# Expert down weights loaded by pairs of experts instead of by halves of rows

## Chip, cores and metric

The kernel runs on one core of a Trainium2 chip. The metric is the device time of one execution in microseconds (us); lower is better. All data are float32.

## What is computed

A decoder trunk of two layers on 256 tokens of width 1024. Each layer adds a mixer (state-space branch and sparse attention), a cross-attention and a hierarchical mixture of experts, and only the last is touched here:

```
for g in range(MOE_GROUPS):                      # 4 groups of 8 experts
    hid = (jax.nn.silu(jnp.einsum('nd,edf->nef', t, w_gate_e[g]))
           * jnp.einsum('nd,edf->nef', t, w_up_e[g]))          # f = 256
    hid = hid * combine[:, g, :, None].astype(hid.dtype)
    out = out + jnp.einsum('nef,efd->nd', hid, w_down_e[g]).astype(F32)
```

A token is routed to one group and there to two of its eight experts. Each expert has gate and up weights of 1024 x 256 and down weights of 256 x 1024, so 1 MB for each of the three.

## The kernel before

The expert part runs in passes. A pass takes one group, with 32 token slots for each of its 8 experts (`S`), in two blocks `b` of four experts (`BE`). Each layer of this run has four passes: the first (`opened`), the second (`early_rows`), the third, and one in a loop over passes (`Fori`) whose count comes from the routing.

What a block does, in TensorE's order (`expert_pass`):

- Gate product (i = 0) and up product (i = 1), line 1263: for each of 8 row chunks k, the four experts j one after the other. The stationary operand has 32 columns, and expert j writes partitions 32j to 32j+31 of a bank, so the four sit side by side on four column groups of the array.
- VectorE and ScalarE make `hid` (128 slots x 256). Two transposes (line 1288) turn its column halves into `hidT`, and ScalarE copies them (line 1559).
- Down product, line 1306: for k = 0, 1 (the half of the 256 rows f), for n = 0, 1 (the half of the 1024 outputs), for the four experts j. Step k reads the buffer `drows[2 * b + k]`: `xs`, `scr` for block 0 and `qq`, `ga` for block 1. (In the second pass `mix_rows` stands for `xs`.) Semaphore `dn_s` rises when k = 0 is over, `ds_s` when each n of k = 1 is over.
- ScalarE copies the sums (line 1565, `yg`), TensorE scatters them back to tokens (line 1323), and VectorE adds them to `h` (line 2220). Before a new pass, VectorE makes the selection (lines 2127, 2196) and TensorE gathers tokens (line 1203). In the first pass the gather for the second is done inside block 1.

All weights are loaded by SP, in one queue, in the order of its program: for each block gate (G), up (U), and the two down buffers (D0, D1). G and U are 4 MB each and go to the two halves of `wring`; a new G may be issued only when the gate product of the block before has read its half (`gu_s`, line 680), likewise U. D0 waits for `dn_s` and D1 for `ds_s` of the pass before (line 671). Since SP waits in order, what is late in front holds everything behind it. Each down buffer is 2 MB: of all four experts of a block, the rows k * 128 to k * 128 + 127, one row of 4 KB for each partition and expert. Gate and up are laid out so that a partition reads 8 KB in one piece.

Of the kernel before, what the change touches and what calls it, by code (L numbers as in the profile page):

```python
# [23 lines left out]
P = 128  # L24
# [251 lines left out]
def trunk(nc, x, mem, w_in, w_ssd_o, w_attn_o, w_out, w_cq, w_ckv, w_co, w_group, w_router,  # L276
          w_gate, w_up, w_down, params, consts, gain_final, out):
    with ExitStack() as ctx:
# [142 lines left out]
        def spare_sums(st):  # L421
# [7 lines left out]
            if st[0] == "atto":  # L429
# [6 lines left out]
        drows = [xs[:, :, :].rearrange("p t (a n) -> p (t a) n", a=2), scr[:, :].rearrange("p (j n) -> p j n", j=BE),  # L436
                 qq[:, :, :].rearrange("p t (a n) -> p (t a) n", a=2), ga[:, :].rearrange("p (j n) -> p j n", j=BE)]
        fgain = cols(mix, 0, D)
        xg_ahead = cols(hT[:, :, :].rearrange("p c t -> p (c t)"), 0, KC, E * S)
        up_ahead = cols(big, 4096, KC * F)  # L440
        gate_ahead = cols(hT[:, :, :].rearrange("p c t -> p (c t)"), 0, KC * F)
# [99 lines left out]
        def drained(eng, l, job):  # L541

            eng.wait_ge(drained_s[OWNER[job]], l * DRAINS[OWNER[job]] + RANK[job])
# [32 lines left out]
        def group_of(engine, i):  # L576

            return number(engine, bass.ds(i, 1), 0, G - 1)
# [15 lines left out]
        def _(sp):  # L594
# [65 lines left out]
                row = acum_rows[l, t, g * HG:(g + 1) * HG, :].rearrange("h s -> (h s)")  # L660
                sp.dma_start(mm_[:, (n + 1) % 2, :], bc(row, 0, P)).then_inc(dec_in[n % 2], 16)

            def down(l, u, g, b, i):

                if i == 0:
                    sp.wait_ge(dn_s, u * NB + (b + 1))
                else:
                    sp.wait_ge(ds_s, u * (2 * NB) + (2 * b + 2))
                settle(sp)
                src = w_down[l, g, b * BE:(b + 1) * BE].rearrange("j (k p) n -> p k j n", p=P)  # L670
                sp.dma_start(drows[2 * b + i][:, :, :], src[:, i]).then_inc(d_in_sem[2 * b + i], 16)

            def up(l, u, g, b, i, first=0):

# [4 lines left out]
                src = (w_gate, w_up)[i][l, g, b * BE:(b + 1) * BE].rearrange("j (p k) n -> p j (k n)", p=P)  # L679
                sp.dma_start(up_part[i][:, first:BE, :], src[:, first:BE, :]).then_inc(up_part_in[i], 16)  # L680

            def experts(l, u, g, down_ahead=(), opening=False):

                for b in range(NB):
                    for i in range(PARTS):
                        if opening and b == 0 and i == 1:

                            sp.wait_ge(gu_s, u * (PARTS * NB) + (i + 1))
                            settle(sp)
                            src = w_up[l, g, 0:BE].rearrange("j (p k) n -> p j (k n)", p=P)  # L690
                            for half, got in enumerate((up_half_in, up_part_in[i])):
                                filled(sp, l, last_job(NCH - PARTS + half))
                                settle(sp)
                                js = slice(half * (BE // 2) + 1 - half, (half + 1) * (BE // 2))
                                if half:
                                    sp.dma_start(up_part[i][:, js, :], src[:, js, :]).then_inc(got, 16)
                                    continue
                                after = w_up[l, g, BE].rearrange("(p k) n -> p (k n)", p=P)
                                sp.dma_start(up_part[i][:, 0, :], after).then_inc(up_next_in, 16)
                                sp.dma_start(up_part[i][:, js, :], src[:, js, :]).then_inc(got, 16)  # L700
                            down(l, u, g, 1, 0)
                            filled(sp, l, JOB[(("router", 1), 0)])
                            settle(sp)
                            after = w_gate[l, g, BE].rearrange("(p k) n -> p (k n)", p=P)
                            sp.dma_start(gate_ahead, after).then_inc(gate_ahead_in, 16)
                            continue
                        if opening and b == 1 and i == 0:

                            src = w_gate[l, g, BE:2 * BE].rearrange("j (p k) n -> p j (k n)", p=P)
                            for half, got in enumerate((gate_half_in, up_part_in[i])):  # L710
                                if half == 0:
                                    sp.wait_ge(gate_half_used, l + 1)
                                else:
                                    sp.wait_ge(gu_s, u * (PARTS * NB) + (PARTS * b + i + 1))
                                settle(sp)
                                ks = slice(half * (KC // 2) * F, (half + 1) * (KC // 2) * F)
                                sp.dma_start(up_part[i][:, 1:BE, ks], src[:, 1:BE, ks]).then_inc(got, 16)
                            continue

                        if not (opening and b == 0):  # L720
                            up(l, u, g, b, i, first=int(opening))
                    for i in range(2):
                        if (b, i) not in down_ahead:
                            down(l, u, g, b, i)

            before = 0
            for l in range(DEPTH):
                sp.wait_ge(prm_used, l + 1)
                settle(sp)
                sp.dma_start(prm[:, :], params[l]).then_inc(prm_in, 16)  # L730
                z0 = CHUNK[(("z", 0), 0)]
                ahead_of = {z0 + 2: (0,), z0 + 4: (1, 2), z0 + 5: (3, 4), z0 + 6: (5, 6), z0 + 7: (7,)}
                for c in range(NCH):
                    if c == CHUNK[(("xbc", 4), 0)]:
                        save_acum(l)
                    for n in ahead_of.get(c, ()):
                        acum_to_all(l, n)
                    chunk(l, c, before)
                    if c == CHUNK[(("cq", 0), 0)]:

                        filled(sp, l, JOB[(("memT", 3), 0)])
                        settle(sp)
                        src = w_down[l, 1, 0:BE].rearrange("j (k p) n -> p k j n", p=P)
                        sp.dma_start(mix_rows, src[:, 0]).then_inc(mix_in, 16)

                        drained(sp, l, JOB[(GATES[3], 4)])
                        settle(sp)
                        sp.dma_start(rw[:, :, 0:G], rows(w_group[l], 0, G)).then_inc(router_in, 16)
                        sp.dma_start(rw[:, :, G:G + G * E], rows(w_router[l], 0, G * E)).then_inc(router_in, 16)

                filled(sp, l, last_job(CHUNK[(("cv", 1), 0)]))
                settle(sp)
                sp.dma_start(up_ahead, w_up[l, 0, 0].rearrange("(p k) n -> p (k n)", p=P)).then_inc(up_ahead_in, 16)
                filled(sp, l, last_job(CHUNK[(("cq", 1), 0)]))
                settle(sp)
                down(l, before, 0, 0, 0)
                up(l, before, 0, 0, 0)
                filled(sp, l, JOB[(("xpv", 3), 0)])
                settle(sp)
                drained(sp, l, JOB[(("cq", 1), 4)])  # L760
                settle(sp)
                down(l, before, 0, 0, 1)
                down(l, before, 0, 1, 1)
                experts(l, before, 0, down_ahead=[(0, 0), (0, 1), (1, 0), (1, 1)], opening=True)
                down(l, before + 1, 1, 0, 1)
                for i in range(1, PLAIN):
                    experts(l, before + i, i, down_ahead=[(0, 0), (0, 1)] if i == 1 else [])
                if l == DEPTH - 1:

                    sp.wait_ge(dn_s, (before + 2) * NB + 1)  # L770
                    settle(sp)
                    sp.dma_start(fgain, gain_final).then_inc(fin_in, 16)
                total, after = passes(sp, SP, l)
                with sp.Fori(PLAIN, total) as i:
                    experts(l, before + i, group_of(SP, i))
                before = after
            for t in range(TT):
                sp.wait_ge((fin_act, fin_s)[t], 1)
# [59 lines left out]
        def _(pe):  # L838
# [379 lines left out]
                    if c % 2:  # L1218
                        ins.then_inc(gat_s, 1)

            def expert_pass(u, spared, opened=False, early_rows=False):

                x = xg_ahead if early_rows else xg
                if opened:
# [8 lines left out]
                for b in range(NB):  # L1233
# [50 lines left out]
                    pe.wait_ge(hid_s, u * NB + (b + 1))  # L1284
                    if opened and b == 0:
                        drained(pe, l, JOB[(("count",), 0)])
                    for k in range(2):
                        ins = nc.tensor.transpose(bank[3][:, k * P:(k + 1) * P], hid[:, b, k * P:(k + 1) * P], ident)
                    ins.then_inc(hT_s, 1)
                    pe.wait_ge(hTc_s, u * NB + (b + 1))  # L1290
                    if opened and b == 1:
# [3 lines left out]
                    for k in range(2):  # L1295
# [6 lines left out]
                        else:  # L1302
                            pe.wait_ge(d_in_sem[0], (u + 1 - spared) * 16)
                        for n in range(2):
                            for j in range(BE):
                                ins = nc.tensor.matmul(bank[4 + n][j * S:(j + 1) * S, :],  # L1306
                                                       hidT[:, b, k * P + j * S:k * P + (j + 1) * S],
                                                       rows[:, j, n * NCOL:(n + 1) * NCOL], start=k == 0, stop=k == 1)
                            if k:
                                ins.then_inc(ds_s, 1)  # L1310
                        if k == 0:
# [16 lines left out]
            for l in range(DEPTH):  # L1328
# [6 lines left out]
                expert_pass(before + 2, l + 1)  # L1335
                total, after = passes(pe, PE, l)
                with pe.Fori(PLAIN, total) as i:
                    expert_pass(before + i, l + 1)
                before = after


# [974 lines left out]
```

## Time and profile before

| | us |
|---|---|
| median of 3 runs | 1497.06 (1496.94 to 1497.62) |
| profiled execution | 1496.66 |
| its span in the trace | 1494.9 |
| TensorE busy | 1376.9 (92%) |
| granted clock, mean | 0.976 of full |
| weights and other HBM reads | 355.89 MB, 239 GB/s over the span |

The span is 1.8 us shorter than the execution's own time. Busy shares are means over stages that differ: in the slices 14 to 19 and 34 to 39 (of 40, counted from 0) the expert passes run, at about 415 GB/s, and in the others products of TensorE bound the kernel. The order of a layer is mixer, cross-attention, experts, so the expert parts lie at about 536 to 743 us and 1275 to 1484 us of the span.

### The profile page before, as it was taken

What the parts mean: (1) busy time and instruction counts of PE and PEld (TensorE: products, weight loads), DVE (VectorE), ACT (ScalarE), POOL (GpSimd) and SP (SyncE); (2) the same over time, 40 slices, a digit from 0 to 9 for tenths busy, and PEclk for the clock granted to TensorE, in tenths of its full rate; (3) what the DMA queues carried; (4) which work ended last, traced back from release to release, by engine and by line L of the source; (5) the groups of instructions that cost most, each with busy time, mean ns of one, the idle gap of its engine ahead of it and who ended that gap; (6) DMA issues with size and microseconds to landing.
All of it is one profiled execution on the core that took longest, in us unless ns stands there. A gap on an engine that the chain in (4) does not pass through costs nothing.

```text
span 1494.9 us, 23994 instructions
## 1 busy us (share of the span) xinstructions
PE 1376.9 (92%) x9670; PEld 1095.7 (73%) x9670; DVE 842.3 (56%) x1605; ACT 383.5 (26%) x867; POOL 70.1 (5%) x65
## 2 busy tenths in 40 slices
PE   8999999999999999767699999999999999978674
PEld 7888888899999654424288888889999996534241
DVE  5477878796875342112265878787958653322022
ACT  2222567421111111001122235576111021111001
POOL 0000420000000000000000014100000000000000
PEclk9999999999999999989999999999999999998998
DMA  9434443353663789999963455433346646999996
GB/s 318 164 119 178 169 156 113 114 197 114 226 229 111 312 352 390 417 415 417 389 223 124 159 183 173 152 114 127 128 149 214 217 187 266 395 389 415 418 417 245
DMA packets 119102, 358.56 MB, mean 240 GB/s; under 512 B 12112, under 2 KB 14544, under 8 KB 103376
## 3 DMA queue, kind: packets, MB, share of 16 engines
q1 hardware_dynamic: 118448, 354.93, 62.6%
q8 instruction: 78, 1.28, 0.4%
q0 software_dynamic: 544, 2.10, 0.4%
q14 instruction: 32, 0.26, 0.1%
HBM read 355.89 MB, written 1.11 MB: 239 GB/s over the span
## 4 chain that ended last, share of the span: by engine, by line
PE 79%; DMA 16%; DVE 2%; issue 1%; SPq 0%; ACT 0%; DVEq 0%; POOL 0%; POOLq 0%; ACTq 0%
PE bank L920 21%; PE bank L923 18%; PE bank L889 13%; DMA ga<-in_w_down_e 11%; DMA wring<-in_w_up_e 5%; PE bank L870 5%; PE bank L1263 5%; PE bank L1203 4%; PE bank L844 3%; PE bank L1040 2%; PE bank L1323 2%; PE bank L1306 1%; PE bank L1129 1%; PE bank L1116 1%; PE bank L1065 1%
## 5 line engine op out<-in xcount | busy, mean ns | idle before, releaser
L889 PE MATMUL bank<-hT,wring 128*128 128x256 f32 x896 | 196.2, 380 | 0.0
L889 PEld LDWEIGHTS bank<-hT,wring 128*128 128x128 f32 x896 | 169.3, 190 | 23.9 <-issue 0.7
L1263 PE MATMUL bank<-wring,big 128*32 128x256 f32 x1472 | 100.7, 421 | 34.7 <-DMA wring<-in_w_up_e 19.9
L2220 DVE TENSOR_TENSOR h<-bank,h 128x512 f32<-128x512 f32 x64 | 44.3, 692 | 116.7 <-PE bank L1323 116.7
L1263 PEld LDWEIGHTS bank<-wring,big 128*32 128x32 f32 x1472 | 50.2, 121 | 76.0 <-DMA wring<-in_w_up_e 22.1
L1816 DVE SCALAR_TENSOR_TENSOR scr<-bank,prm,scr 128x255 f32<-128x255 f32 (+1 forms) x144 | 62.7, 477 | 46.8 <-ACT scr L1389 44.0
L2211 DVE TENSOR_TENSOR big<-bank,big 128x256 f32<-128x256 f32 x16 | 6.8, 425 | 143.9 <-ACT big L1555 143.9
L920 PE MATMUL bank<-hT,wring 128*128 128x128 f32 x736 | 86.9, 276 | 0.8 <-DVE btok L1673 0.8
L920 PEld LDWEIGHTS bank<-hT,wring 128*128 128x128 f32 x736 | 84.2, 192 | 3.4 <-issue 2.1
L1203 PE MATMUL bank<-big,xn 128*128 128x256 f32 x256 | 72.5, 439 | 12.5 <-DVE big L2127 12.3
L1354 ACT ACTIVATE ga<-bank 128x256 f32<-128x256 f32 x48 | 18.4, 384 | 247.6 <-PE bank L920 173.0
L1203 PEld LDWEIGHTS bank<-big,xn 128*128 128x128 f32 x256 | 65.5, 335 | 22.0 <-DVE big L2127 16.0
L920 PE MATMUL bank<-big,wring 128*128 128x128 f32 x704 | 80.9, 275 | 0.0
L920 PEld LDWEIGHTS bank<-big,wring 128*128 128x128 f32 x704 | 79.9, 192 | 0.1
L923 PE MATMUL bank<-wring,hT 128*128 128x256 f32 x336 | 77.1, 379 | 0.0
L923 PE MATMUL bank<-wring,xn 128*128 128x256 f32 x320 | 72.3, 379 | 0.0
L923 PEld LDWEIGHTS bank<-wring,hT 128*128 128x128 f32 x336 | 63.5, 190 | 11.0 <-issue 2.9
L923 PEld LDWEIGHTS bank<-wring,xn 128*128 128x128 f32 x320 | 60.6, 190 | 11.6 <-issue 3.8
L1323 PE MATMUL bank<-big 128*128 128x512 f32 x128 | 62.2, 618 | 0.1
L1643 DVE TENSOR_TENSOR wring<-wring 128x1024 f32<-128x1024 f32 (+1 forms) x44 | 59.6, 1354 | 1.2
L870 PE MATMUL bank<-wring,qq 128*128 128x512 f32 x128 | 56.9, 595 | 0.0
L1555 ACT ACTIVATE big<-bank 128x256 f32<-128x256 f32 x16 | 6.2, 385 | 192.4 <-PE bank L1263 192.4
(370 smaller groups left out, 2333.6 us busy)
## 6 DMA issues: line engine op xcount, KB each, us to landing
wring<-in_w_in SPq DMA_DIRECT2D x68, 1024.0 KB, 7.2
wring<-in_w_gate_e SPq DMA_DIRECT2D x14, 4096.0 KB, 18.1
wring<-in_w_up_e SPq DMA_DIRECT2D x12, 4096.0 KB, 23.6
wring<-in_w_ssd_o SPq DMA_DIRECT2D x16, 1024.0 KB, 6.2
wring<-in_w_ckv SPq DMA_DIRECT2D x16, 1024.0 KB, 7.3
scr<-in_w_down_e SPq DMA_DIRECT2D x8, 2048.0 KB, 22.6
ga<-in_w_down_e SPq DMA_DIRECT2D x8, 2048.0 KB, 29.2
qq<-in_w_down_e SPq DMA_DIRECT2D x8, 2048.0 KB, 24.7
```

The source lines that it names most:

```text
L844: ins = nc.tensor.transpose(b[:, i * P:(i + 1) * P], src, ident)
L870: ins = nc.tensor.matmul(bank[bank_of(job)][:, 0:width], src[:, k, t * P:(t + 1) * P], wring[:, SLOT[c], k, 0:width], start=i == 0, stop=i ...
L889: ins = nc.tensor.matmul(bank[bank_of(job)][:, i * SEQ:(i + 1) * SEQ], wring[:, SLOT[c], k, m:m + P], src[:, k, :], start=n == 0, stop=n = ...
L920: ins = nc.tensor.matmul(b[:, i * P:(i + 1) * P], w[:, j, i * P:(i + 1) * P], x[:, j, :], start=j == 0, stop=j == k - 1)
L923: ins = nc.tensor.matmul(b[:, 0:HALF_W], x[:, j, :], w[:, j, :], start=j == 0, stop=j == k - 1)
L1040: ins = nc.tensor.matmul(bank[bank_of(job)][:, i * SP_:(i + 1) * SP_], mm_[:, (n + 1) % 2, i * P:(i + 1) * P], xdt[:, n % 2, i * SP_:(i + ...
L1203: return nc.tensor.matmul(bank[banks[c // 2]][:, (c % 2) * E * S:(c % 2 + 1) * E * S], xn_eighth[:, k, c, :], sel[:, k, :], start=start, s ...
L1263: ins = nc.tensor.matmul(bank[b][j * S:(j + 1) * S, i * F:(i + 1) * F], x[:, k, e:e + S], w[:, k * F:(k + 1) * F], start=k == 0, stop=k == ...
L1323: nc.tensor.matmul(bank[6 + n][:, :], selT[:, b, k * P:(k + 1) * P], yg[:, n * NCOL:(n + 1) * NCOL], start=True, stop=True).then_inc(sct_s, 1)
L1643: V.tensor_tensor(out, a, b, ALU.subtract).then_inc(wsum_rdy, 1)
L1816: ins = V.scalar_tensor_tensor(conv[:, m % 2, i, k:SEQ], b[:, i * SEQ:(i + 1) * SEQ - k], prm[:, w:w + 1], conv[:, m % 2, i, k:SEQ], ALU.m ...
L2220: V.tensor_tensor(hh, bank[6 + n][:, :], hh, ALU.add).then_inc(add_s, 1)
```

## The change

Down weights now come by pairs of experts. Buffer `drows[2 * b + i]` holds the whole down weights of the experts 2i and 2i+1 of its block, and partition p holds rows 2p and 2p+1 of each, which lie one behind the other in memory: 8 KB in one piece. The same 2 MB go to the same buffer at the same place of SP's order. Only block 1 of the looped pass keeps the old form.

On TensorE the transposes take every second column of `hid` instead of the first and second 128. Step k of the down product now does the whole of two experts: for each n, row half 0 for both, then row half 1 for both. Block 1 of the looped pass keeps the old order.

```diff
+        def pair_rows(rows):
+            return rows.rearrange("p (j k) n -> p j (k n)", k=2)
...
+            def down_pair(l, g, b, i):
+                e = b * BE + 2 * i
+                return w_down[l, g, e:e + 2].rearrange("j (p k) n -> p j (k n)", p=P)
...
-            def down(l, u, g, b, i):
+            def down(l, u, g, b, i, pairs=True):
...
-                src = w_down[l, g, b * BE:(b + 1) * BE].rearrange("j (k p) n -> p k j n", p=P)
-                sp.dma_start(drows[2 * b + i][:, :, :], src[:, i]).then_inc(d_in_sem[2 * b + i], 16)
+                if pairs:
+                    dst, src = pair_rows(drows[2 * b + i]), down_pair(l, g, b, i)
+                else:
+                    dst = drows[2 * b + i][:, :, :]
+                    src = w_down[l, g, b * BE:(b + 1) * BE].rearrange("j (k p) n -> p k j n", p=P)[:, i]
+                sp.dma_start(dst, src).then_inc(d_in_sem[2 * b + i], 16)
...
-                            down(l, u, g, b, i)
+                            down(l, u, g, b, i, pairs=not (looped and b))
...
-                        src = w_down[l, 1, 0:BE].rearrange("j (k p) n -> p k j n", p=P)
-                        sp.dma_start(mix_rows, src[:, 0]).then_inc(mix_in, 16)
+                        sp.dma_start(pair_rows(mix_rows), down_pair(l, 1, 0, 0)).then_inc(mix_in, 16)
...
+                    pairs_in = not (looped and b)
                     for k in range(2):
-                        ins = nc.tensor.transpose(bank[3][:, k * P:(k + 1) * P], hid[:, b, k * P:(k + 1) * P], ident)
+                        part = hid[:, b, :].rearrange("p (q k) -> p k q", k=2)[:, k] if pairs_in else hid[:, b, k * P:(k + 1) * P]
+                        ins = nc.tensor.transpose(bank[3][:, k * P:(k + 1) * P], part, ident)
...
-                            for j in range(BE):
+                            steps = ([(2 * k + a, j, 2 * a + j) for j in range(2) for a in range(2)] if pairs_in
+                                     else [(j, k, j) for j in range(BE)])
+                            for j, half, row in steps:
                                 ins = nc.tensor.matmul(bank[4 + n][j * S:(j + 1) * S, :],
-                                                       hidT[:, b, k * P + j * S:k * P + (j + 1) * S],
-                                                       rows[:, j, n * NCOL:(n + 1) * NCOL], start=k == 0, stop=k == 1)
+                                                       hidT[:, b, half * P + j * S:half * P + (j + 1) * S],
+                                                       rows[:, row, n * NCOL:(n + 1) * NCOL], start=half == 0, stop=half == 1)
```

On SP, from the down load that the first pass triggers to the two of the second pass, before (4 experts x 1024 elements for each partition in a down load):

```order
L671 DMA scr<-in_w_down_e 128x4x1024
L680 DMA wring<-in_w_gate_e 128x4x2048
L680 DMA wring<-in_w_up_e 128x4x2048
L680 DMA wring<-in_w_gate_e 128x4x2048
L680 DMA wring<-in_w_up_e 128x4x2048
L671 DMA qq<-in_w_down_e 128x4x1024
L671 DMA ga<-in_w_down_e 128x4x1024
```

and now:

```order
L685 DMA scr<-in_w_down_e 128x2x2048
L694 DMA wring<-in_w_gate_e 128x4x2048
L694 DMA wring<-in_w_up_e 128x4x2048
L694 DMA wring<-in_w_gate_e 128x4x2048
L694 DMA wring<-in_w_up_e 128x4x2048
L685 DMA qq<-in_w_down_e 128x2x2048
L685 DMA ga<-in_w_down_e 128x2x2048
```

No load has moved; each down load has half as many pieces, twice as long.

On TensorE, the down product and the scatter of the first pass's block 0, before:

```order
L1288 MATMUL bank3<-cst,big 128x128 x2
L1306 MATMUL bank4<-xs,big 32x512 x4
L1306 MATMUL bank5<-xs,big 32x512 x4
L1306 MATMUL bank4<-scr,big 32x512 x4
L1306 MATMUL bank5<-scr,big 32x512 x4
```

and now:

```order
L1303 MATMUL bank3<-cst,big 128x128 x2
L1323 MATMUL bank4<-xs,big 32x512 x4
L1323 MATMUL bank5<-xs,big 32x512 x4
L1323 MATMUL bank4<-scr,big 32x512 x4
L1323 MATMUL bank5<-scr,big 32x512 x4
```

The count of products and their banks are the same. What the rows don't show is that each group of four went to the column groups 0, 1, 2, 3 before and goes to 0, 1, 0, 1 (`xs`) and 2, 3, 2, 3 (`scr`) now.

## Rows read from the trace of the kernel before

**Rows 1.** The page's 40 slices of the span, in tenths; last row the moved GB/s.

```profile
PE   8999999999999999767699999999999999978674
...
GB/s 318 164 119 178 169 156 113 114 197 114 226 229 111 312 352 390 417 415 417 389 223 124 159 183 173 152 114 127 128 149 214 217 187 266 395 389 415 418 417 245
```

**Rows 2.** Chain that ended last, layer 0: start us, us, engine, line; matmuls and weight loads counted.

```profile
547.84 3.64 PE bank L1306 x32
...
566.71 17.52 DMA wring<-in_w_up_e
...
644.02 33.38 DMA ga<-in_w_down_e
```

**Rows 3.** PE, first pass: start us, us, line, out<-in, form, count [idle before <-releaser].

```profile
547.84 1.92 PE L1306 MATMUL bank<-xs,big 128*32 128x512 f32 x16 [0.47 <-ACT big L1559]
549.58 1.90 PE L1306 MATMUL bank<-scr,big 128*32 128x512 f32 x16
551.43 3.87 PE L1323 MATMUL bank<-big 128*128 128x512 f32 x8
...
571.93 1.92 PE L1306 MATMUL bank<-qq,big 128*32 128x512 f32 x16 [0.98 <-ACT big L1559]
573.68 1.90 PE L1306 MATMUL bank<-ga,big 128*32 128x512 f32 x16
...
579.33 3.66 PE L1263 MATMUL bank<-wring,hT 128*32 128x256 f32 x64
```

**Rows 4.** PE in order of time: a product on two column groups.

```profile
253.09 1.08 PE L1085 MATMUL bank<-qq,mix 128*64 128x512 f32 x4
```

**Rows 5.** Windows of 2 us: us, busy of PE, PEld, DVE, ACT, POOL; clock, DMA share, GB/s.

```profile
580.00:582.00 2.00, 2.00 (x44) 1.23 (x40) 0.89 (x3) 0.00 (x0) 0.00 (x0) 1.00 0.87 365
582.00:584.00 2.00, 1.58 (x24) 0.75 (x16) 0.39 (x1) 0.00 (x0) 0.00 (x0) 1.00 0.23 90
584.00:586.00 2.00, 1.73 (x32) 1.07 (x36) 0.31 (x1) 0.00 (x0) 0.00 (x0) 1.00 0.92 254
```

**Rows 6.** The queue of SP, issues of weight loads: start us, us, line.

```profile
559.01 0.37 SPq L680 DMA_DIRECT2D wring<-in_w_gate_e  x1
...
583.11 0.37 SPq L680 DMA_DIRECT2D wring<-in_w_gate_e  x1
...
701.97 0.37 SPq L680 DMA_DIRECT2D wring<-in_w_gate_e  x1
...
1322.82 0.37 SPq L680 DMA_DIRECT2D wring<-in_w_gate_e  x1
...
1440.22 0.37 SPq L680 DMA_DIRECT2D wring<-in_w_gate_e  x1
```

**Rows 7.** Windows as in rows 5, in streams of gate/up (1, 3) and down (2, 4).

```profile
708.00:724.00 16.00, 10.98 (x104) 4.07 (x99) 2.76 (x4) 1.20 (x2) 0.00 (x0) 1.00 1.01 421
726.00:734.00 8.00, 5.67 (x66) 2.58 (x66) 0.42 (x1) 0.39 (x1) 0.00 (x0) 0.70 1.02 409
1448.00:1464.00 16.00, 10.76 (x92) 4.02 (x88) 2.77 (x4) 1.20 (x2) 0.00 (x0) 0.89 1.01 419
1468.00:1476.00 8.00, 6.16 (x74) 2.86 (x78) 0.42 (x1) 0.77 (x2) 0.00 (x0) 0.79 1.03 410
```

**Rows 8.** Weight loads by line and form: busy us, mean ns, idle before.

```profile
L1203 PEld LDWEIGHTS bank<-big,xn 128*128 128x128 f32 x256 | 65.5, 335 | 22.0 <-DVE big L2127 16.0 <-issue 3.3
L1288 PEld LDWEIGHTS bank<-cst,big 128*128 128x128 f32 x32 | 3.4, 142 | 20.4 <-DVE big L2211 20.3
```

**Rows 9.** PE in order of time: down product of the third pass, block 1, both layers.

```profile
675.45 1.92 PE L1306 MATMUL bank<-qq,big 128*32 128x512 f32 x16 [0.47 <-ACT big L1559]
677.44 1.92 PE L1306 MATMUL bank<-ga,big 128*32 128x512 f32 x16
...
1413.98 1.92 PE L1306 MATMUL bank<-qq,big 128*32 128x512 f32 x16 [0.47 <-ACT big L1559]
1417.22 1.92 PE L1306 MATMUL bank<-ga,big 128*32 128x512 f32 x16 [1.32 <-DMA ga<-in_w_down_e]
```

More of the change, by code:

```diff
@@ L680, in up, with experts @@
                 sp.dma_start(up_part[i][:, first:BE, :], src[:, first:BE, :]).then_inc(up_part_in[i], 16)
-            def experts(l, u, g, down_ahead=(), opening=False):
+            def experts(l, u, g, down_ahead=(), opening=False, looped=False):
                 for b in range(NB):
@@ L774, in _ @@
                 with sp.Fori(PLAIN, total) as i:
-                    experts(l, before + i, group_of(SP, i))
+                    experts(l, before + i, group_of(SP, i), looped=True)
                 before = after
@@ L1219, in gather_both, with expert_pass @@
                         ins.then_inc(gat_s, 1)
-            def expert_pass(u, spared, opened=False, early_rows=False):
+            def expert_pass(u, spared, opened=False, early_rows=False, looped=False):
                 x = xg_ahead if early_rows else xg
@@ L1337, in _ @@
                 with pe.Fori(PLAIN, total) as i:
-                    expert_pass(before + i, l + 1)
+                    expert_pass(before + i, l + 1, looped=True)
                 before = after
```

## Prediction

> **What bounds the kernel now.** I read the page's slices first. The expert parts (slices 14 to 19 and 34 to 39) move about 415 GB/s and every other part moves far less [rows 1]. There the DMA engines look like the bound, and the change shortens pieces of just these loads. But the change also rearranges the down product on TensorE, so the second question is where in the expert part TensorE is the bound. The chain that ended last answers it: from 547.84 to 566.7 us it is TensorE's alone, then it goes over to landings of gate, up and down weights, with waits of 17 to 33 us [rows 2]. So a layer's expert part has two regimes. In the first pass, whose weights were mostly loaded ahead, TensorE runs from product to product. From the second pass on the stream of 24 MB a pass decides.
>
> The seam between the two is where the price of this change is set. SP may issue the gate load of the second pass's block 1 only after the gate product of that pass's block 0, which runs from 579.33 to 583.0 [rows 3], and the issue stands at 583.11 [rows 6]. By then the queue has run dry: the DMA share is 0.87, 0.23 and 0.92 in the three windows of 2 us from 580 on [rows 5]. Taking the missing shares, that is 2.0 us of nothing. So here the stream waits for TensorE: whatever makes TensorE later in the first pass makes this issue later, and all that comes behind, up to the last down load of the layer, is one stream that then has no more gap to take it up. This is the point at which a microsecond of TensorE is a microsecond of the kernel.
>
> **Pieces of 8 KB.** The last two down loads of a layer run alone, in pieces of 4 KB: 409 and 410 GB/s. Streams of gate and up alone, in pieces of 8 KB: 421 and 419 GB/s [rows 7]. 2 MiB are 2.097 MB: 5.12 us at 409.5, 4.99 us at 420, so a down load saves 0.13 us (from 421 against 409, 0.15; from 419 against 410, 0.11). Behind the seam, eight changed down loads per layer follow: qq and ga of the second pass, four of the third, xs and scr of the looped one. 8 x 0.13 = 1.05 us per layer. The loads before the seam (four for the first pass, two for the second's first block) are hidden: TensorE decides there. Two layers: **-2.1 us**, bounds -1.8 and -2.4.
>
> A rule speaks against even this. The Trainium skill, "DMA: Bandwidth & Descriptors", Specifications, puts the least size for line rate at 512 B, so that 4 KB and 8 KB would do the same. Rows 7 disagree by 2.5%; going by the rule the saving would be nothing.
>
> **The down product on half the array.** Before, the four experts of a block stand on four column groups and run side by side. The trace shows it: 16 instructions of 512 columns take 1.92 us, and step k = 1 starts 1.74 us after k = 0 (547.84 to 549.58, [rows 3]), so four rounds of 4 instructions, 0.43 us a round. Now step k holds two experts, in the order a, b, a, b. Equal groups must follow each other, so a round is 2 instructions and there are 8 rounds a step. The trace has such a product: on two column groups, 4 instructions of 512 columns take 1.08 us [rows 4], which is two rounds of 0.43 and a tail. So 8 rounds are 3.47 us instead of 1.74, and a block with both steps costs 16 rounds, +3.47 us. At the seam of the two steps the groups differ (0, 1, then 2, 3), so the second step may start beside the last round of the first: up to 0.3 us back. I take **+3.3 us per block**; bounds: 1.7 (if half of it overlaps, for which no row speaks) and 3.5.
>
> Where does it count? In the first pass both blocks' down products lie in the unbroken run of TensorE: 547.84 and 571.93 [rows 3]; behind each, scatter, products and gather follow with no idle time over 1 us, and none of them for a load. 2 x 3.3 = 6.6 us later at the seam. One step earlier the same delay meets the gate load at 559.01 [rows 6]; it comes 3.3 us later and starves the stream some 2 us, but the loads behind it end at 584 or so, before the new issue at 583.1 + 6.6 = 589.7, so it isn't added. The gap at the seam grows from 2 us to about 8.6. **+6.6 us per layer, +13.2 in both** (the same issue stands at 1322.82 in layer 1 [rows 6]). In the later passes TensorE waits for loads soon after a down product, and behind block 0's product the next G is issued with both down loads of block 1 and most of U still ahead of it in the queue: over 10 us of stream at 420 GB/s, against 3.3 us. So nothing there.
>
> **The looped pass's seam.** The one later place that is tight is the same issue one pass on: the gate load of block 1 in the looped pass. Layer 0: the third pass's last down load lands at 644.02 + 33.38 = 677.4 [rows 2]. Landing is seen about 2 us after the queue ends with it. Behind it G, U, xs, scr are queued, 12.6 MB, 30.2 us at 416. A new load needs 1.7 us to flow (583.11 to about 584.8, [rows 5, 6]). So the new G must be issued by 677.4 - 2.0 + 30.2 - 1.7 = 703.9; it is at 701.97 [rows 6]: 1.9 us of slack. The third pass's block 1 starts its two steps at 675.45 and 677.44 [rows 9]; with 3.47 us each, they end 3.0 us later than now. 1.1 us are short, and the faster xs and scr take 0.3 more: the stream waits 1.2 us or so, bounds 0 and 1.6. Layer 1: steps at 1413.98 and 1417.22 [rows 9], so k = 0 is just over when the second load lands, and only +1.8 us remain, against a slack of 1417.2 - 2.0 + 30.2 - 1.7 - 1440.22 = 3.5. Nothing. **+1.2 us.** The last block of the layer keeps the old order, so the tail behind the last landing stays.
>
> **Transposes.** They now read every second column of `hid` as stationary operand, two per block, on TensorE's path in the first pass. The trace has no such load. The contiguous ones of now have a mean of 142 ns; the gather's loads, which take every eighth column, 335 ns [rows 8]. So between nothing and 4 x 0.19 = 0.8 us per layer (two blocks, two exposed each). I take 0, since a step of two columns is nearer to one than to eight; bound +1.5 in both layers.
>
> The Trainium skill, "SBUF — State Buffer", the note on cachelines under "Door 1: The DMA port swizzle", says lines of 16 bytes with two hits in each run at full rate. A stride of two floats has two hits, the gather's one; rows 8 agree for the latter, and no row here shows the former. By that rule the transposes cost 0, as in the sum.
>
> **Sum.** Against the profiled execution of 1496.66 (span 1494.9), 0.4 us below the median: -2.1 + 13.2 + 1.2 = +12.3 us. On the median of 1497.06: **1509.4 us**, own range 1506 to 1513 from the bounds without the overlap.
>
> **Rivals.**
> 1. TensorE overlaps the two row halves of an expert in part, so that a block costs 1.7 us. Then the seam moves 3.4 us a layer, the looped pass's seam nothing: 6.8 - 2.1 = +4.7, 1501.8 us. Against it: rows 4, where alternate groups take full rounds.
> 2. The down product costs nothing at the seam, since something else that I take for idle sets the gate issue. Then only the pieces count: -2.1, 1495.0 us, which is within 0.2%; to be faster by over 3 us a load would have to save 0.19 us, half as much again as rows 7 give. That decides if the issue at 583.11 doesn't move. Against it: it follows the product's end by 0.1 us in the trace.
> 3. Pieces of 8 KB bring nothing for these loads, as if they were moved as 4 KB: no -2.1, 1511.5 us. Against it: rows 7. It is what the rule above from the Trainium skill, "DMA: Bandwidth & Descriptors", would give.
> 4. The pass seams get worse than summed: strided transposes at the upper bound, the looped seam short in both layers and a lower clock after the longer waits: +3 to +5 more, 1513 to 1515 us.
>
> **Chances.** Forecast 0.67, rival 1 0.10, rival 2 0.09 (of it 0.03 faster), rival 3 0.08, rival 4 0.06. A measurement of this kernel tells about 0.2% (3 us) from no change. Slower 0.91, same 0.06, faster 0.03. The range leaves out rival 2 and the most of rival 4: 1501 to 1513.
>
> **What would show it.** In the changed profile: the 16 down instructions of `xs` take about 3.6 us instead of 1.92; block 0's scatter in the first pass starts near 554.8 and block 1's near 582; the second pass's second gate issue stands at about 589.7, with the DMA share near zero for 8 us ahead of it; behind it, streams of down loads at 420 GB/s; the chain holds TensorE up to 573 instead of 566.7. The forecast is wrong if the down product of 16 instructions stays under 2.5 us, or if that gate issue stays at 583.

## The result, and the profile after

| | us | lowest to highest; of the ratio, 95% interval |
|---|---|---|
| before, median of 7 | 1497.06 | 1495.98 to 1497.62 |
| after, median of 7 | 1501.74 | 1500.95 to 1503.28 |
| ratio after / before | 1.0033 | 1.0024 to 1.0042 |
| profiled execution, after | 1501.32 (span 1499.5) | |

The kernel became slower by 4.7 us, 0.33%. The direction was forecast, the size was not: 12.3 us were. The median lies below the own range of 1506 to 1513 us, and at the very foot of the wide one of 1501 to 1513, which only rival 1 reached.

TensorE in order of time around the down product of the first pass's block 0, after the change (start us, us, engine, line, form, count; line 1323 is the down product, 1340 the scatter):

```profile
549.05 2.34 PE L1323 MATMUL bank<-xs,big 128*32 128x512 f32 x10 [0.47 <-ACT big L1576]
550.80 0.62 PE L1323 MATMUL bank<-scr,big 128*32 128x512 f32 x2
551.22 0.60 PE L1323 MATMUL bank<-xs,big 128*32 128x512 f32 x2
551.26 0.60 PE L1323 MATMUL bank<-scr,big 128*32 128x512 f32 x2
552.08 0.60 PE L1323 MATMUL bank<-xs,big 128*32 128x512 f32 x2
552.12 2.31 PE L1323 MATMUL bank<-scr,big 128*32 128x512 f32 x10
554.36 1.98 PE L1340 MATMUL bank<-big 128*128 128x512 f32 x4
```

This answers to [rows 3]. The products of `xs` (experts 0 and 1) start at 549.05 and those of `scr` (experts 2 and 3) already at 550.80, 1.75 us later, while `xs` still goes on, two instructions a round, until 552.08 and a round more. From 550.80 on two on `xs` and two on `scr` run beside each other. The scatter starts 5.31 us after the first product, where it was 3.59 us before: a block costs +1.7 us, not +3.3.

The queue of SP, the gate loads that answer to [rows 6]:

```profile
561.96 0.37 SPq L694 DMA_DIRECT2D wring<-in_w_gate_e  x1
587.82 0.37 SPq L694 DMA_DIRECT2D wring<-in_w_gate_e  x1
...
1328.96 0.37 SPq L694 DMA_DIRECT2D wring<-in_w_gate_e  x1
```

From the first down product (549.05) to the second gate issue of the second pass (587.82) are 38.77 us. Before, it was 583.11 - 547.84 = 35.27 [rows 3, 6]: +3.50 us, of which the two blocks' products make 1.72 and 1.73. The chain of waits gives the same stations (start us, us, engine, line), after:

```profile
549.05 5.38 PE bank L1323 x32
554.43 3.82 PE bank L1340 x8
...
588.30 3.63 PE bank L1276 x64
592.00 19.38 DMA wring<-in_w_up_e
...
741.61 1.92 PE bank L1323 x16
...
1289.94 5.38 PE bank L1323 x32
...
1483.33 1.92 PE bank L1323 x16
```

and before:

```profile
737.60 1.92 PE bank L1306 x16
...
751.55 10.78 PE bank L870 x64
...
1287.26 3.64 PE bank L1306 x32
...
1478.55 1.92 PE bank L1306 x16
```

In layer 1 the same stretch is 1328.96 - 1289.94 = 39.02 against 1322.82 - 1287.26 = 35.56 [rows 6]: +3.46 us. The chain stays with TensorE until 592.00, where it left it at 566.71 [rows 2] and 573 were forecast. Before, TensorE reached the up product of that block 0.70 us ahead of its load's landing (584.27), and so the chain went back along that load:

```profile
584.27 3.66 PE L1263 MATMUL bank<-wring,hT 128*32 128x256 f32 x64 [0.70 <-DMA wring<-in_w_up_e]
```

Now TensorE comes after the landing.

From the second gate issue to the product behind the last landing of the layer: 741.61 - 587.82 = 153.79 against 737.60 - 583.11 = 154.49, so -0.70 us; in layer 1 154.37 against 155.73, -1.36 us. There the saving of the longer pieces is seen.

Windows after the change (us, busy of PE, PEld, DVE, ACT, POOL, clock, DMA share, GB/s):

```profile
584.00:586.00 2.00, 2.00 (x37) 1.20 (x40) 1.45 (x3) 0.00 (x0) 0.00 (x0) 1.00 0.17 70
586.00:588.00 2.00, 2.00 (x35) 1.14 (x28) 0.00 (x0) 0.00 (x0) 0.00 (x0) 1.00 0.04 12
588.00:590.00 2.00, 2.00 (x39) 1.15 (x41) 0.69 (x1) 0.00 (x0) 0.00 (x0) 1.00 0.49 135
670.00:678.00 8.00, 5.85 (x66) 2.98 (x66) 0.42 (x1) 0.48 (x2) 0.00 (x0) 0.79 1.02 424
712.00:728.00 16.00, 13.30 (x106) 5.01 (x106) 3.11 (x5) 1.58 (x3) 0.00 (x0) 1.00 1.01 424
708.00:712.00 4.00, 3.44 (x64) 1.82 (x56) 0.66 (x2) 0.38 (x1) 0.00 (x0) 1.00 1.02 369
```

Three things answer to [rows 5] and [rows 7]. The queue is dry for longer at the first pass's seam: shares of 0.17, 0.04 and 0.49 in three windows of 2 us, 4.6 us without load in these alone. Down loads are no longer told from gate and up loads: 424 GB/s from 670 to 678, in front of the landing at 681.0 of the third pass's last down load, and 424 from 712 on, where gate and up load. And there is a short gap at the looped pass's seam in layer 0, 369 GB/s from 708 to 712.

**What of the profile is no part of the change.** The first product of the layer's experts stands 1.21 us later than before (549.05 against 547.84), though nothing before it was changed but how a few loads are cut. Of this, 0.07 us are the strided transposes (experiment 3). In the five experiments whose code is the same up to there (all but 2 and 3) the product stands between 547.94 and 548.94, so the most of it is a difference between executions. And the start of layer 1 came 1.3 us earlier, against the product behind the last landing: before, its first large product is at 751.55 (13.95 us behind 737.60), after, at

```profile
754.25 10.72 PE bank L883 x64
```

12.64 us behind 741.61. Here the granted clock tells why. Before:

```profile
748.00:752.00 4.00, 3.90 (x21) 3.88 (x22) 1.75 (x4) 1.25 (x4) 0.00 (x0) 0.60 1.05 387
```

and after, in the same stretch of the program:

```profile
752.00:756.00 4.00, 3.69 (x32) 3.51 (x32) 1.66 (x4) 2.72 (x5) 0.00 (x0) 1.00 1.05 387
```

0.60 is a mean over 4 us between the two levels, 1.2 and 2.4 GHz. Before the window TensorE had waited for VectorE and ScalarE (1.61 us busy out of 4 in the window before, after the change 1.62), and in one execution the clock fell there and in the other it did not; what decides it, these rows don't show. Of the seven experiments' profiled executions one has the short stretch too, that of experiment 6, with a granted clock of 1.00 there; the six others have the long one, with 0.57 to 0.66 over the 4 us in question. So +1.2 and -1.3 cancel to 0.1, and the difference of the profiled executions, 4.66 us, is made by 3.50 - 0.70 + 3.46 - 1.36 = 4.9 us, less 0.2 at the end.

### The profile page after: what moved, and what is told of

Its sections match the earlier page's. It is cut to its first block, busy times and chain, and to the rows that moved or that the text cites. A ratio compares the mean times of both kernels' runs of the same rounds, so it can differ in the third digit from the quotient of the medians.

```text
span 1499.5 us, 23994 instructions
## 1 busy us (share of the span) xinstructions
PE 1403.0 (94%) x9670; PEld 1106.2 (74%) x9670; DVE 842.5 (56%) x1605; ACT 383.0 (26%) x867; POOL 71.1 (5%) x65
## 4 chain that ended last, share of the span: by engine, by line
PE 85%; DMA 10%; DVE 3%; issue 1%; ACT 1%; DVEq 0%; SPq 0%; POOL 0%; ACTq 0%; POOLq 0%
PE bank L933 21%; PE bank L936 18%; PE bank L902 13%; PE bank L1276 6%; DMA wring<-in_w_up_e 6%; PE bank L883 5%; PE bank L1216 5%; DMA ga<-in_w_down_e 4%; PE bank L1323 3%; PE bank L857 3%; PE bank L1340 3%; PE bank L1053 2%; PE bank L1142 1%; PE bank L1129 1%; PE bank L1078 1%
## 5 line engine op out<-in xcount | busy, mean ns | idle before, releaser
L1216 PE MATMUL bank<-big,xn 128*128 128x256 f32 x256 | 72.4, 439 | 12.5 <-DVE big L2144 12.3
L801 POOL TENSOR_TENSOR sums<-sums,cst 128x2 f32<-128x2 f32 (+2 forms) x13 | 10.6, 818 | 937.9 <-DVE sums L1613 353.4
```

Of the source, the lines that this page charges most:

```text
L1216: return nc.tensor.matmul(bank[banks[c // 2]][:, (c % 2) * E * S:(c % 2 + 1) * E * S], xn_eighth[:, k, c, :], sel[:, k, :], start=start, s ...
```

## Experiments

All are edits of the changed kernel. Medians are compared with the 1501.74 of the changed kernel and the 1497.06 of the one before, whose medians beside the experiments were 1497.06 (1 to 4) and 1496.98 (5 to 7). The ratios are to these, with a 95% interval.

### 1. Four column groups in each round

```diff
+                    if pairs_in:
+                        ... # waits for both loads of the block
+                        for n in range(2):
+                            for half in range(2):
+                                for e in range(BE):
+                                    rows = mix_rows if early_rows and b == 0 and e < 2 else drows[2 * b + e // 2]
+                                    ins = nc.tensor.matmul(bank[4 + n][e * S:(e + 1) * S, :],
+                                                           hidT[:, b, half * P + e * S:half * P + (e + 1) * S],
+                                                           rows[:, 2 * (e % 2) + half, n * NCOL:(n + 1) * NCOL],
+                                                           start=half == 0, stop=half == 1)
```

> The changed kernel, but where down weights come by pairs the product waits for both loads of a block and then goes through all four experts for each row half, so that each round stands on four column groups again. Theory A (the loss comes from the down product of the first pass's two blocks on two groups at a time): a block's 32 instructions take 3.6 us as before the change instead of 5.4, the second pass's second gate issue comes back by 3.5 us relative to the start of the layer's expert part, and the pieces' saving of 2.1 us is left: 1495.0 us, 1493.5 to 1496.5. Theory B (the loss comes from the new layout itself, such as the loads' landing or the strided transposes): the time stays near 1501.5 us.

Measured: 1496.32 us (1495.37 to 1497.92, 11 runs), ratio to before 0.9994 (0.9985 to 1.0003). TensorE in the first pass, and the gate issue of the seam:

```profile
548.20 0.62 PE L1322 MATMUL bank<-xs,big 128*32 128x512 f32 x2 [0.47 <-ACT big L1595]
548.21 0.62 PE L1322 MATMUL bank<-scr,big 128*32 128x512 f32 x2
...
551.23 0.60 PE L1322 MATMUL bank<-xs,big 128*32 128x512 f32 x2
551.24 0.60 PE L1322 MATMUL bank<-scr,big 128*32 128x512 f32 x2
551.77 1.55 PE L1359 MATMUL bank<-big 128*128 128x512 f32 x3
...
583.47 0.37 SPq L694 DMA_DIRECT2D wring<-in_w_gate_e  x1
```

Two instructions on `xs` and two on `scr` start together from the first round on, the scatter follows after 3.57 us, and the gate issue is 583.47 - 548.20 = 35.27 us behind the first product, in layer 0 to the hundredth as before the change (in layer 1 35.68 against 35.56). So the seam's whole delay sits in these products. The time is 1.3 us above what I expected, inside the range, and the trace shows one reason: with both loads waited for, the looped pass's seam of layer 0 is dry for longer, a share of 0.93 and 338 GB/s in

```profile
704.00:708.00 4.00, 3.81 (x66) 1.98 (x64) 0.69 (x1) 0.13 (x1) 0.00 (x0) 1.00 0.93 338
```

so that from the second gate issue to the product behind the last landing it saves 0.0 us in layer 0 (737.94 - 583.47 = 154.47, against 154.49), but 1.4 us in layer 1 (154.37 against 155.73).

### 2. The first pass in the old form

```diff
-                down(l, before, 0, 0, 0)
+                down(l, before, 0, 0, 0, pairs=False)
...
-                    pairs_in = not (looped and b)
+                    pairs_in = not (looped and b or opened)
```

(and so for the first pass's three other down loads.)

> The changed kernel, with the four down loads and the two down products of the first pass in the old form (4 KB pieces, four groups). Theory A: only these two blocks cost time, the blocks of the later passes are hidden behind loads: 1495.0 us, 1494 to 1497, and the second pass's second gate issue stands where it did before the change. Theory B (the later passes lose as well, by products that end 1.8 us later behind the last landing and by a queue that runs dry in the looped pass): 1498 to 1500 us.

Measured: 1495.10 us (1493.23 to 1497.18, 11 runs), ratio 0.9987 (0.9978 to 0.9996). Theory A. The first pass's product and the gate issue of the seam:

```profile
548.36 1.92 PE L1323 MATMUL bank<-xs,big 128*32 128x512 f32 x16 [0.47 <-ACT big L1576]
...
583.63 0.37 SPq L694 DMA_DIRECT2D wring<-in_w_gate_e  x1
```

That is 35.27 us again, as before the change. With the first pass alone taken back, 6.6 us come back, and what is left of the change is a gain of 2.0 us: what pieces of 8 KB save where loads bound the kernel, less what the later passes' new order costs there.

### 3. Pairs in pieces of 4 KB

```diff
-                return w_down[l, g, e:e + 2].rearrange("j (p k) n -> p j (k n)", p=P)
+                return w_down[l, g, e:e + 2].rearrange("j (k p) n -> p (j k) n", p=P)
...
-            return rows.rearrange("p (j k) n -> p j (k n)", k=2)
+            return rows
...
-                        part = hid[:, b, :].rearrange("p (q k) -> p k q", k=2)[:, k] if pairs_in else hid[:, b, k * P:(k + 1) * P]
+                        part = hid[:, b, k * P:(k + 1) * P]
```

> The changed kernel with its pairs of experts and its order of products, but each buffer takes the rows k * 128 + p, in pieces of 4 KB, and the transposes are contiguous again. Theory A (pieces of 8 KB save 0.13 us a load behind the seam, transposes cost nothing): 1501.7 + 2.1 = 1503.8 us, 1503 to 1505. Theory B (pieces make no difference): 1501.7. Theory C (strided transposes cost more than the pieces save): under 1501 us.

Measured: 1504.33 us (1503.62 to 1504.67, 5 runs), ratio 1.0046 (1.0032 to 1.0060). Theory A: the order of products alone costs 7.3 us, and pieces of 8 KB, with the strided transposes that come with them, give 2.6 us of it back (2.1 expected). Behind the seam this kernel takes what the one before took, 154.49 us in layer 0 and 155.67 in layer 1 (154.49 and 155.73), so there the order of products alone costs nothing that the trace shows, and what the changed kernel saves there is by its pieces. The same run prices the strided transposes. Contiguous, here (line 1303 is the transposes):

```profile
548.10 0.44 PE L1303 MATMUL bank<-cst,big 128*128 128x128 f32 x2 [0.96 <-DVE big L2228]
549.01 2.34 PE L1323 MATMUL bank<-xs,big 128*32 128x512 f32 x10 [0.47 <-ACT big L1576]
550.76 0.62 PE L1323 MATMUL bank<-scr,big 128*32 128x512 f32 x2
```

0.91 us from the transposes to the first product; strided, in the changed kernel, weight loads of this line have a mean of 197 ns instead of 142 [rows 8], 28 of the 32 being strided (so about 205 ns for a strided one; in experiment 7, where all 32 are, the mean is 206):

```profile
L1303 PEld LDWEIGHTS bank<-cst,big 128*128 128x128 f32 x32 | 5.0, 197 | 20.3 <-DVE big L2228 20.3
```

and the way takes 0.98 us (548.07 to 549.05). So 0.07 us for block 0 of a first pass. Block 1's transposes lie beside a wait for ScalarE's copies and cost nothing: from the first down product to the seam's gate issue are 38.78 us with contiguous ones and 38.77 with strided ones. That makes 0.14 us in both layers. The Trainium skill, "SBUF — State Buffer", the note on cachelines under "Door 1: The DMA port swizzle", would have had a stride of two floats cost nothing; the measurement says some 60 ns a load, small, but not nothing.

### 4. Step 1 only after step 0

```diff
+                        if opened and k:
+                            pe.wait_ge(dn_s, u * NB + (b + 1) + NB)
```

> The changed kernel, and in the first pass step 1 of a block's down product waits until step 0 is over. Theory A (in the changed kernel step 1 starts on its own two groups 1.75 us after step 0, while half of step 0 still waits for its groups, and so a block costs 1.75 us instead of 3.4): a block now takes 7.1 us instead of 5.4, each layer's seam moves by another 3.4 us: 1501.7 + 6.9 = 1508.6 us, 1507 to 1510. Theory B (a block's time is set otherwise, and the steps' overlap is only how the trace models ends): 1501.7 us.

Measured: 1510.49 us (1509.60 to 1511.42, 4 runs), ratio 1.0091 (1.0075 to 1.0106).

```profile
548.05 3.63 PE L1325 MATMUL bank<-xs,big 128*32 128x512 f32 x16 [0.47 <-ACT big L1578]
551.84 3.63 PE L1325 MATMUL bank<-scr,big 128*32 128x512 f32 x16 [0.16 <-PE bank L1325]
555.40 3.89 PE L1342 MATMUL bank<-big 128*128 128x512 f32 x8
...
590.87 0.37 SPq L694 DMA_DIRECT2D wring<-in_w_gate_e  x1
```

This is the kernel that the prediction had priced: steps one after the other, each of 8 rounds, 3.63 us. A block takes 7.35 us to the scatter instead of 5.31, so 2.04 us more, of which 1.7 are the overlap and 0.3 the wait itself. Four blocks make 8.2 us; by medians 8.75 were measured, 0.5 us above the range, and between the profiled executions (1509.60 and 1501.32) 8.3. With the overlap forbidden the loss against before is 13.4 us, near the 13.2 + 1.2 - 2.1 = 12.3 of the prediction. So theory A's cause holds, though its range was missed by the wait's own price: what the sum lacked is that step 1 starts on its own two groups while step 0 still waits for its groups.

### 5. One expert after the other

```diff
+                        if opened:
+                            for a in range(2):
+                                for n in range(2):
+                                    for half in range(2):
+                                        e = 2 * k + a
+                                        ins = nc.tensor.matmul(...)   # as before, on group e
```

> The changed kernel, and in the first pass a step goes through one expert after the other: 8 instructions on one column group, then 8 on the next. Theory A1 (each column group holds three instructions that wait for it, and TensorE goes past them to other groups): an expert's products start four rounds of 0.43 us after those of the one before, at 0, 1.74, 3.47 and 5.2 us, and a block takes 8.9 us instead of 5.4; two blocks in two layers: +13.9 us, 1515.6 us, 1513 to 1518. Theory A2 (six may wait in all, whatever their group): starts at 0, 0.4, 2.2 and 3.9 us or so, a block takes about 7.4 us, 1509.7 us. Theory A3 (TensorE goes past nothing that waits): a block takes 13.9 us, 1535 us.

Measured: 1515.46 us (1515.26 to 1515.89, 4 runs), ratio 1.0123 (1.0108 to 1.0139).

```profile
547.94 4.08 PE L1324 MATMUL bank<-xs,big 128*32 128x512 f32 x13 [0.47 <-ACT big L1587]
551.43 0.62 PE L1324 MATMUL bank<-scr,big 128*32 128x512 f32 x1
551.85 0.59 PE L1324 MATMUL bank<-xs,big 128*32 128x512 f32 x1
...
552.71 0.59 PE L1324 MATMUL bank<-xs,big 128*32 128x512 f32 x1
552.74 4.05 PE L1324 MATMUL bank<-scr,big 128*32 128x512 f32 x13
556.73 3.46 PE L1351 MATMUL bank<-big 128*128 128x512 f32 x7
```

Expert 2 (the first on `scr`) starts at 551.43, 3.49 us behind expert 0 (3.47 by theory A1, 2.2 by A2), and the products end 8.85 us after the first starts (8.9 by A1). The rows from 551.43 to 552.71 also show expert 1's and expert 2's products side by side, one and one. Expert 1 is merged with expert 0 in the first row; narrower views have one instruction on `xs` at 549.25 and two from 549.68 on, 1.74 us behind the first, again as in A1 (0.4 by A2). So in these runs TensorE goes past an instruction that waits for a busy column group, and each group holds three that wait; the fourth stops everything behind it. One limit for all groups together doesn't fit both kernels: here three wait when the next group's first gets by, in the changed kernel six. The three is worked out from these starts; what in TensorE holds them, the runs don't show. In the changed kernel that is just what sets 1.75 us: a step has 8 instructions for each of its groups, and the ninth, the other step's first, gets by when the eighth is among the three that wait, which is when the fifth starts, four rounds in.

### 6. Four groups in the first pass only

Experiment 1 with `if opened:` in place of `if pairs_in:`, so that the later passes are those of the changed kernel.

> The changed kernel, pairs and 8 KB everywhere as there, but in the first pass alone the product goes through four experts for each row half. Theory A: the seam of the first pass is that of the kernel before, and behind it all is as in the changed kernel: 3.5 us less per layer, 1501.7 - 7.0 = 1494.7 us, 1493.5 to 1496, so the same as with the first pass in halves (1495.1). Theory B (the later passes with steps on two groups cost more than with four groups, or the other way): away from 1494.7 by over 1 us, towards 1496.3, which four groups everywhere gave.

Measured: 1494.75 us (1493.92 to 1496.92, 11 runs), ratio 0.9988 (0.9979 to 0.9997). The lowest median here; it and experiment 2 (1495.10) are the only ones faster than before beyond the interval, by 2.2 and 2.0 us. It is also 1.6 us under experiment 1, whose later passes wait for both loads of a block before the first product; the samples of the two overlap, so how much of the 1.6 us that waiting costs is not settled. In the profiled executions layer 0 behind the seam takes 153.26 us here and 154.47 there, and experiment 1's window shows the place.

### 7. Pairs in the looped pass's block 1 too

```diff
-                            down(l, u, g, b, i, pairs=not (looped and b))
+                            down(l, u, g, b, i, pairs=True)
...
-                    pairs_in = not (looped and b)
+                    pairs_in = True
```

> The changed kernel, with the looped pass's block 1 in pairs too. Theory A: behind the last landing of a layer stand 8 rounds on two groups instead of 4 on four, +1.73 us, and two more loads save 0.13 us each, so +1.5 us per layer and 1501.7 + 3.0 = 1504.7 us, 1503.5 to 1506. Theory B (the tail is hidden behind the scatter and the next layer's first work): 1501.7 or 0.5 us less.

Measured: 1504.43 us (1504.24 to 1505.96, 5 runs), ratio 1.0051 (1.0038 to 1.0065). The end of layer 0:

```profile
738.19 2.34 PE L1323 MATMUL bank<-qq,big 128*32 128x512 f32 x10 [0.47 <-ACT big L1576]
740.22 0.62 PE L1323 MATMUL bank<-ga,big 128*32 128x512 f32 x2
...
741.54 2.31 PE L1323 MATMUL bank<-ga,big 128*32 128x512 f32 x10
743.78 3.95 PE L1340 MATMUL bank<-big 128*128 128x512 f32 x8
```

Behind the last landing (740.22) the scatter starts after 3.56 us, where the old form has 1.93 (741.61 to 743.54 in the changed kernel). These products lie on the chain that ended last, so all of it counts: 2.7 us in both layers, with the saving of four more loads taken off. This is what the exception for that block avoids.

## Why the prediction was right in direction and wrong in size

- **Where the price is set: right.** The second gate issue of the second pass moved by 3.50 and 3.46 us, of which the two blocks' products of the first pass make 3.45 and 3.40, and it went through to the end of each layer. Experiments 2 and 6, which touch the first pass alone, bring it back to 35.27 and 35.26 us in layer 0 (35.27 before).
- **The down product on half the array: the term that was mis-sized.** The step "at the seam of the two steps the groups differ, so the second step may start beside the last round of the first: up to 0.3 us back" took the overlap for one round. It is four rounds: a block costs 1.7 us, not 3.3, so 7.0 us in all instead of 13.2. [rows 4] showed rightly that two groups take full rounds, but its four instructions could not show what stands in the queue behind them. The bound of 1.7 was in the text, tied to an overlap of row halves; experiment 4 shows that it is the overlap of the steps. Rival 1 had the time (1501.8) for the wrong cause, and a chance of 0.10. The prediction's signs did not test the overlap: 16 instructions on `xs` do take 3.6 us, as it said, and neither sign of being wrong came, yet the seam's gate issue stood 38.77 us behind the first product where about 41.9 were forecast, and its queue was dry for some 4.6 us, not 8.6.
- **Pieces of 8 KB: right, somewhat more than summed.** -1.36 us in layer 1 against -1.05, or 0.17 us a load instead of 0.13 (0.15 to 0.17 in experiments 1, 2, 4, 5 and 6); by medians 2.6 us between experiment 3 and the changed kernel. The Trainium skill, "DMA: Bandwidth & Descriptors", Specifications, asks only for 512 B, and by that 4 KB and 8 KB would run alike; these runs don't bear that out, nor rival 3.
- **The looped pass's seam: right in place, its size not settled.** In the changed kernel's trace layer 0 saves 0.66 us less than layer 1, and a window of it shows 369 GB/s; 1.2 us were forecast, within bounds of 0 to 1.6 (its two parts, 1.1 and 0.3, make 1.4). Layer 1 shows no such loss, as forecast. But experiments 2, 4, 5 and 6, whose later passes are the same, save 0.58, 1.03, 0.98 and 1.23 us in layer 0 in one execution each, so the loss lies between nothing and 0.8 us and differs by execution. With pieces of 4 KB (experiment 3) there is none.
- **Transposes:** 0.14 us, between the bounds of 0 and 1.5.
- **Rival 4** adds up to 1512.4 to 1514.4 us, not 1513 to 1515; nothing hangs on it.
- With the sizes of the profiled executions the sum is 7.0 - 2.7 + 0.7 + 0.1 = 5.1 us, against 4.7 measured.

## What to carry to other kernels

A change that makes transfers cheaper and products dearer is to be judged stage by stage: here it gained 2 us where loads bound the kernel and lost 7 us in the one pass where TensorE bound it, and either form of the repair (the old layout there, or four column groups there) left the gain alone. When products stand on separate column groups of the array, price them by the longest run of instructions on one group and by what may pass them, not by rounds put end to end; and keep neighbouring instructions on different groups. In front of a last landing keep the form whose products behind it are shortest.

## What the runs showed of the hardware that was not expected

- TensorE's instructions for a free column group pass those that wait for a busy one, until three wait for a group. The second step started 1.75 us after the first (four rounds of 0.43 us) with six instructions of the first still to run; with one group at a time, the second expert started 1.74 us and the third 3.49 us after the first. So products do not start in the order of the program.
- A semaphore wait of TensorE on its own last product costs about 0.3 us (experiment 4).
- Weight loads of 128 x 128 with a step of two floats take about 205 ns, against 142 ns without and 335 ns in the gather, with a step of eight [rows 8].
- The same code up to the first expert product took from 547.94 to 549.05 us in six profiled executions, and the clock at the start of layer 1 makes another 1.3 us; a single profiled execution doesn't tell a change of a microsecond.
